# Router logits taken from the residual rows before their norm, with rows transposed one column half at a time

## What is computed

```
def rms_norm(x, gain):
    y = x32 * lax.rsqrt(jnp.mean(x32 * x32, axis=-1, keepdims=True) + EPS)
    return (y * gain.astype(jnp.float32)).astype(x.dtype)
...
        x = x + hybrid_mixer(h, ...)                 # ends with y @ w_out
        h = rms_norm(x, norm_ffn_gain[l])
        x = x + hierarchical_moe(h, w_router_group[l], b_router_group[l], w_router_expert[l], ...)
...
    group_p = jax.nn.softmax((t @ w_router_group) + b_router_group, axis=-1)
    exp_logits = ((t @ w_router_expert) + b_router_expert).reshape(n_tok, N_GROUPS, EXPERTS_PER_GROUP)
```

## Time and profile before

| | us |
|---|---|
| median of 3 runs (774.04, 775.37, 775.72) | 775.37 |
| the profiled execution, its own time | 773.31 |
| its span, first to last instruction | 771.6 |
| PE busy | 699.9 (91%) |
| VectorE busy | 334.7 (43%) |
| ScalarE busy | 288.7 (37%) |
| GpSimd busy | 199.5 (26%) |
| mean granted TensorE clock | 0.963 |

### The profile page before, as it was taken

One profiled execution on the slowest core, in us unless ns is written; L12 is line 12 of the kernel. 1 busy time (PEld: TensorE's weight loads), 2 busy tenths in 40 slices (PEclk: granted clock), 3 DMA queues, 4 the chain that ended last, 5 costly groups with the idle time before them and its releaser, 6 DMA issues.

```text
span 771.6 us, 10997 instructions
## 1 busy us (share of the span) xinstructions
PE 699.9 (91%) x4258; PEld 513.4 (67%) x4258; DVE 334.7 (43%) x612; ACT 288.7 (37%) x533; POOL 199.5 (26%) x171
## 2 busy tenths in 40 slices
PE   3999999998999999999999996699999999997830
PEld 3688888886878798888778886454455545454520
DVE  4349897979684423564478136500000000000008
ACT  6313655671444653565543131221222223131203
POOL 2045433431341231442552000212222121211110
PEclk9999999999999999999999996699999999999985
DMA  8913333030030020206741329889999999999726
GB/s 238 345 62 128 110 110 109 15 137 14 28 124 14 3 109 1 110 1 232 313 144 57 151 108 405 346 344 400 418 398 419 397 418 398 419 418 418 318 107 250
DMA packets 45122, 164.66 MB, mean 213 GB/s; under 512 B 9420, under 2 KB 13532, under 8 KB 32270
## 3 DMA queue, kind: packets, MB, share of 16 engines
q1 hardware_dynamic: 39758, 155.52, 52.1%
q0 software_dynamic: 5312, 8.42, 3.1%
HBM read 154.09 MB, written 19.53 MB: 225 GB/s over the span
## 4 chain that ended last, share of the span: by engine, by line
PE 82%; DVE 6%; ACT 4%; issue 3%; DMA 2%; POOL 2%; POOLq 0%; DVEq 0%; ACTq 0%
PE bank L961 14%; PE bank L467 13%; PE bank L469 12%; PE bank L468 12%; PE bank L995 7%; PE bank L958 5%; PE bank L940 3%; PE bank L989 2%; PE bank L595 2%; PE bank L972 2%; DVE arena L2364 1%; PE bank L858 1%; PE bank L626 1%; PE bank L616 1%; PE bank L798 1%
## 5 line engine op out<-in xcount | busy, mean ns | idle before, releaser
L1247 POOL TENSOR_TENSOR w_lo<-arena,w_hi 128x1024 fp32r<-128x1024 f32 x36 | 86.1, 2396 | 209.3 <-ACT w_hi L1410 209.3
L467 PE MATMUL bank<-h_hi,w_hi 128*128 128x512 f32 x320 | 128.3, 401 | 0.4 <-DVE arena L1953 0.4
L469 PE MATMUL bank<-h_hi,w_lo 128*128 128x512 f32 x320 | 125.0, 391 | 0.0
L468 PE MATMUL bank<-h_lo,w_hi 128*128 128x512 f32 x320 | 124.6, 389 | 0.0
L961 PE MATMUL bank<-arena 128*64 128x256 f32 x896 | 106.5, 392 | 8.4 <-issue 7.2
L961 PEld LDWEIGHTS bank<-arena 128*64 128x64 f32 x896 | 65.7, 140 | 39.0 <-issue 9.4
L2318 DVE TENSOR_TENSOR arena<-arena,bank 64x256 f32<-64x256 f32 x28 | 11.6, 412 | 180.8 <-ACT arena L1758 180.8
L1865 DVE SCALAR_TENSOR_TENSOR bank<-arena,bank 128x512 f32<-128x512 f32 x116 | 78.7, 749 | 0.1
L1371 POOL DMA_INDIRECT y_rows<-arena,row_half x28 | 28.0, 998 | 167.9 <-ACT arena L1779 167.9
L469 PEld LDWEIGHTS bank<-h_hi,w_lo 128*128 128x128 f32 x320 | 60.1, 188 | 13.1
L467 PEld LDWEIGHTS bank<-h_hi,w_hi 128*128 128x128 f32 x320 | 60.1, 188 | 12.9 <-DVE arena L1953 0.6
(11 more groups left out here) (355 smaller groups left out, 1131.7 us busy)
## 6 DMA issues: line engine op xcount, KB each, us to landing
arena<-in_w_expert_down_dram SPq DMA_DIRECT2D x33, 1024.0 KB, 20.7
arena<-in_w_expert_gate_dram SPq DMA_DIRECT2D x33, 1024.0 KB, 19.1
arena<-in_w_expert_up_dram SPq DMA_DIRECT2D x33, 1024.0 KB, 23.0
arena<-in_w_in_dram SPq DMA_DIRECT2D x8, 2048.0 KB, 8.1
arena<-in_x_dram SPq DMA_DIRECT2D x8, 512.0 KB, 7.3
arena<-in_w_in_dram SPq DMA_DIRECT2D x4, 1024.0 KB, 10.6
y_rows<-arena SPq DMA_DIRECT2D x8, 512.0 KB, 10.3
arena<-in_w_out_dram SPq DMA_DIRECT2D x2, 2048.0 KB, 10.2
```

The lines of the kernel that those rows point to most:

```text
L467: pe.matmul(o, wh, xh, start=first, stop=False)
L468: pe.matmul(o, wh, xl, start=False, stop=False)
L469: return pe.matmul(o, wl, xh, start=False, stop=last)
L1247: gp.tensor_tensor(as_raw(w_lo[pslot(s)], s), raw(s), as_raw(w_hi[pslot(s)], s).bitcast(F32), ALU.subtract)\
```

## The change

The logits are linear in the normed row, and the norm is one factor per token. So the changed kernel transposes the residual rows themselves, folds the gain into the router weights (one VectorE multiplication `wr * gcol`, with the gain loaded once more as a column per block of 128), and multiplies the finished logits by the reciprocal root, token by token (`logits_of`). Since a column half of a row is now enough for half of the transposes, PE transposes half tiles, `turn(c, half)`, behind the third product step (`m == 2`) of a later projection group in both passes, and multiplies whole tiles of logits behind the seventh (`m == 6`) in the second pass. ScalarE squares halves, and the sum of the first half enters the root as its bias. The normed rows `h2` are still made and stored, for the gather.

```diff
             def turn(c, half):
+                b = begin(("xT", c, half), copied(c, half))
+                wait(pe, "x1_ready", (1 - half) * NT + c + 1)
+                for k in range(KH):
+                    kk = half * KH + k
+                    ins = pe.transpose(b[:, k * P:(k + 1) * P], x1[:, c, kk * P:(kk + 1) * P], ident)
+                end(ins, ("xT", c, half), "route_mm")
+
+            def logits_half(c, half):
+                if half == 1:
+                    begin(("logits", c), ("x1_ready", NT + c + 2) if c < NT - 1 else ("routed", 1))
+                    held.append(jobs["logits", c][0])
+                    wait(pe, "wr_ready", 1)
...
+                for k in range(half * KH, half * KH + KH):
+                    ins = pe.matmul(b[:, 0:NL], h2T[:, k, c * P:(c + 1) * P], wr_wide[k],
+                                    start=(k == KH), stop=(k == KH - 1))
...
+                        if m == 2 and (p, c) != (0, 0):
+                            turn((c - 1) % NT, 1 if p == 0 or c == 0 else 0)
+                        if m == 6 and p == 1 and c > 0:
+                            logits_half(c - 1, 1)
+                            logits_half(c - 1, 0)
                     end(ins, ("wo", c, hf), "wo_mm")
-                    if p == 1 and c > 0:
-                        h2_tile(c - 1)
-                    if p == 1 and c > 1:
-                        logits_tile(c - 2)
-
-            logits_tile(NT - 2)
-            h2_tile(NT - 1)
-            logits_tile(NT - 1)
-            held.clear()
+            logits_half(NT - 1, 1)
+            turn(NT - 1, 0)
+            logits_half(NT - 1, 0)
...
-            sp.dma_start(wr[:, :, 0:NG], a["w_router_group"][0].rearrange("(p k) n -> p k n", k=KT)).then_inc(S["ld_part2"], 16)
-            sp.dma_start(wr[:, :, NG:NR], a["w_router_expert"][0].rearrange("(p k) n -> p k n", k=KT)).then_inc(S["ld_part2"], 16)
+            sp.dma_start(wr[:, :, 0:NG], a["w_router_group"][0].rearrange("(k p) n -> p k n", p=P)).then_inc(S["ld_part2"], 16)
+            sp.dma_start(wr[:, :, NG:NR], a["w_router_expert"][0].rearrange("(k p) n -> p k n", p=P)).then_inc(S["ld_part2"], 16)
+            sp.dma_start(gcol, a["norm_ffn_gain"][0].rearrange("(k p) -> p k", p=P), allow_slow_non_contiguous=True).then_inc(S["ld_part2"], 16)
...
-            v.wait_ge(S["ld_part2"], 48)
+            v.wait_ge(S["ld_part2"], 64)
+            TT(wr, wr, bc(gcol.unsqueeze(2), [P, KT, NR]), ALU.mult).then_inc(S["wr_ready"], 1)
             v.wait_ge(S["yc_mm"], KT)
...
+            def logits_of(c):
+                src = ready(v, ("logits", c))
+                return STT(out=lg[:, c, :], in0=src[:, 0:NR], scalar=sm["r2"][:, c:c + 1], in1=rbias,
+                           op0=ALU.mult, op1=ALU.add)
+
             for c in range(NT):
+                if c > 0:
+                    logits_of(c - 1)
                 add_half(c, 0)
...
-            tell(TT(lg, src[:, 0:NT * NL].rearrange("p (c n) -> p c n", c=NT)[:, :, 0:NR], bc(rbias.unsqueeze(1), [P, NT, NR]),
-                    ALU.add), "routed")
+            tell(logits_of(NT - 1), "routed")
```

More of the change, by code:

```diff
@@ L251, in hybrid_layer @@
         gain2 = at(R_S2, D)
+        gcol = g1
         gain3 = at(slot_at[HOME[3]], D)
@@ L827, in _ @@
                 end(ins, ("yd", m), "yd_mm")
-            def normed(c):
-                return "h2_ready", c + 1 + (c == NT - 1)
             def copied(c, half):
[L834 to L852, removed]
-                    wait(pe, "rconst", 1)
[L854 to L860, removed]
+                if half == 1:
+                    return "h2T_ready", c + 1
@@ new lines, in copied, with turn @@
+                return ("h2T_ready", NT + c + 1) if c < NT - 1 else ("h2_ready", NT)
+            def turn(c, half):
+                b = begin(("xT", c, half), copied(c, half))
[5 more added lines that the diff above has]
+            def logits_half(c, half):
+                if half == 1:
+                    begin(("logits", c), ("x1_ready", NT + c + 2) if c < NT - 1 else ("routed", 1))
+                    held.append(jobs["logits", c][0])
+                    wait(pe, "wr_ready", 1)
+                    wait(pe, "rconst", 1)
+                b = bank[jobs["logits", c][0]]
+                wait(pe, *copied(c, half))
+                for k in range(half * KH, half * KH + KH):
+                    ins = pe.matmul(b[:, 0:NL], h2T[:, k, c * P:(c + 1) * P], wr_wide[k],
+                                    start=(k == KH), stop=(k == KH - 1))
+                if half == 0:
+                    end(ins, ("logits", c), "route_mm")
+                    held.clear()
@@ L1164, in _ @@
             expert_dn(fixed[4], 4)
-            wait(sp, *jobs["logits"][1:])
+            wait(sp, *jobs["logits", NT - 1][1:])
             expert_dn(fixed[0], 0)
@@ L1714, in _, with xT_copy @@
             act.wait_ge(S["yc_ready"], 2 * KT)
[L1716 to L1732, removed]
+            def xT_copy(c, half):
+                tell(act.activation(h2T[:, KH * half:KH * half + KH, c * P:(c + 1) * P],
+                                    ready(act, ("xT", c, half)).rearrange("p (k n) -> p k n", k=KH), ACT.Copy),
+                     "h2T_ready")
+            for p, (hf, part) in enumerate(((1, "s1"), (0, "ss2"))):
+                for c in range(NT):
+                    act.wait_ge(S["x1_ready"], p * NT + c + 1)
+                    if p + c > 0:
+                        act.wait_ge(S["ss"], (p + 1) * NT + c)
+                    act.activation(junk[:, 0:HALF], x1[:, c, hf * HALF:(hf + 1) * HALF], ACT.Square,
+                                   accum_out=sm[part][:, c:c + 1]).then_inc(S["ss"], 1)
+                    if p == 1:
+                        act.wait_ge(S["ss"], 2 * NT + c + 1)
+                        if c == 0:
+                            act.wait_ge(S["x1_ready"], NT + 1)
+                            act.wait_ge(S["half_ss"], 1)
+                        act.activation(sm["ss2"][:, c:c + 1], sm["ss2"][:, c:c + 1], ACT.Sqrt, scale=1.0 / D,
+                                       bias=sm["s2"][:, c:c + 1]).then_inc(S["rms"], 1)
+                    if (p, c) != (1, NT - 1):
+                        xT_copy(c, hf)
             act.wait_ge(S["route_dif"], 1)
@@ L2350, in _ @@
             v.engine_nop().then_inc(S["ov_over"], 1)
-            v.wait_ge(S["ld_part2"], 64)
+            v.wait_ge(S["ld_part2"], 80)
             def final(c):
```

15 lines of the change are left out of this document (8 added, 7 removed).

## The result

The changed kernel takes 782.05 us (median of four runs, 781.43 to 782.59), the kernel before, on the same chip, 775.29 (774.04 to 775.72). The ratio is 1.0088 [1.0067, 1.0109]: **6.8 us slower**. The direction was forecast, the size was not: 2.7 us were predicted, and the range ended at 781.2.

A forecast was written before the change was run, and what follows sets the result against it. PE bounds the projection, expert-weight DMA the stretch from 510 to 711, with the routing deciding the end. Terms 5.3 + 1.4 - 4.0 = +2.7 us on the median 775.37 gave 778.1 us; range 774.8 to 781.2.

The forecast's parts named there:

- PE work in front of the last group, +5.3: Projection: more transposes and logits tiles on PE before its last group lengthen it by 5.3 us (4.8 to 5.8).
- the wait, +1.4: Projection's first pass: PE's first transposes wait for the first `add_half`, about 1.4 us (0.9 to 1.7).
- The rival that they would be hidden: Projection: moved PE work slips in cheaply between products; sum -2.6 to -1.0 us, 772.8 to 774.4 us; chance 0.15.
- The tail, -4.0: From the projection's last product to the selection: 4.1 us in place of 8.05, so -4.0 us (-3.4 to -4.4).
- The end of the run moves by what the selection's first instruction moves.: Routing to end: while the DMA queue still runs dry there, the run's end shifts as the selection does, +2.7 us.
- a rival with a chance of 0.10: First gather: sharing engines with more queued weights, it lands later, +3.0 us more, 781.1 us; chance 0.10.
- kept the queues full until the gather landed: Behind the projection: the nine weight loads filled the queues until the gather landed; they now wait 6.7 us longer.
- The +3.0 from the median of all gathers: First gather: if it took the median of all gathers, 8.9 us, in place of 5.92, +3.0 us more.
- The stream's floor, +1.8: Weight stream: loads 6.7 us later, 4.9 us of idle time absorbed; end at least 1.8 us later even without routing shift.
- the window 492 to 511: Around the first experts: sign to look for, DMA still runs dry once between 492 and 511 us.

The follow-up runs named there:

- no_stall: Changed kernel with the projection's first transposes behind the sixth product step instead of the third, where their sum is ready; 779.62 us, ratio 1.0056.
- before_hold2: Kernel before, with two weight loads (down of experts 0 and 4) issued behind the first gather's landing instead of in front of it; 775.73 us, ratio 0.9999.
- late_turns: Changed kernel with all transposes and logits behind the projection, except tile 0's transposes in its last group; copies on ScalarE; 772.87 us, ratio 0.9957.
- hold2: Changed kernel, with two weight loads (down of experts 0 and 4) issued behind the first gather's landing instead of in front of it; 777.06 us, ratio 1.0028.
- hold2_no_stall: Changed kernel with both edits: first transposes three product steps later, and two weight loads held behind the first gather; 777.40 us, ratio 1.0020.
- late_selection: Changed kernel with eight small VectorE additions, never read, in front of the selection; 781.19 us, ratio 1.0082.
- more_queued: Changed kernel with the three loads of expert 1 (3 MB) issued in front of the first gather instead of behind its landing; 779.89 us, ratio 1.0080.
- before_late_stream: Kernel before, with the nine weight loads after the projection issued behind the end of the logits instead of the last projection group; 778.89 us, ratio 1.0040.

## Why the prediction was right in direction and wrong in size

*PE work in front of the last group, +5.3, and the wait, +1.4.* Together 6.7; measured 6.55. The price of an insertion was right: of the 6.55, the wait took 1.37 to 1.58 (below), which leaves 5.0 to 5.2 for the moved work, and the chain has 0.44 for four transposes and 1.73 for a tile of logits. The rival that they would be hidden is refuted: its -1.0 at most against +2.31 at the selection. PE's last product before the first transposes, these, and VectorE's part of the wait:

```profile
422.81 0.39 PE L470 MATMUL bank<-wo_hi,ylo 128*128 128x512 f32 x1
...
424.56 0.63 PE L841 MATMUL bank<-arena 128*128 128x128 f32 x4 [1.37 <-DVE arena L2149]
```

```profile
418.81 4.63 DVE L2108 TENSOR_TENSOR wo_lo<-arena,wo_hi 128x1024 fp32r<-128x1024 f32 x4 [0.26 <-ACT wo_hi L1675]
...
423.37 0.45 DVE L2143 TENSOR_TENSOR arena<-arena 128x288 f32<-128x288 f32 x1
423.73 0.68 DVE L2149 TENSOR_TENSOR arena<-arena,bank 128x512 f32<-128x512 f32 x1
```

The idle time is 1.37 us, for 1.4 predicted; the new product `wr * gcol` took 0.45, for 0.4. In no_stall, without the wait, the last product came 1.58 earlier.

*The tail, -4.0.* From 469.53, where the chain leaves the projection (460.78 in the earlier trace rows), to the selection at 473.34 it is 3.81 us, for 4.1 predicted; the earlier trace rows show the same stretch of before.

```profile
469.56 0.69 DVE L2149 TENSOR_TENSOR arena<-arena,bank 128x512 f32<-128x512 f32 x1 [0.49 <-PE bank L470]
471.06 0.69 DVE L2170 COPY arena<-bank 128x512 f32<-128x512 f32 x1 [0.81 <-PE bank L841]
...
471.86 1.28 DVE L2175 SCALAR_TENSOR_TENSOR arena<-arena 128x1024 f32<-128x1024 f32 x1
473.06 0.25 DVE L2161 SCALAR_TENSOR_TENSOR arena<-bank,arena 128x36 f32<-128x36 f32 x1
473.34 0.17 DVE L2187 TENSOR_REDUCE arena<-arena 128x4 f32<-128x16 f32 x1
```

The normed row stands directly before the last logits, as foreseen. So the selection's shift, 6.55 - 4.24 = +2.31, was right within 0.4 us.

*"The end of the run moves by what the selection's first instruction moves."* **This step failed.** It held the gather's landing at 5.92 us, and priced the other case as a rival with a chance of 0.10. That rival was the truth: 9.45 us, +3.5. The argument against it was that "the slices around the first gather are full of weights before too, and it took 5.92 all the same". A slice of the page is 19 us long. Two-microsecond stretches would have shown that the share was falling to 0.74 as the gather landed. The sentence that the nine loads "kept the queues full until the gather landed" was wrong for the same reason: their queue was empty 2 us before. The prediction also had both numbers from which the collision follows, and did not set them against each other: the loads move 6.7 us and the gather 2.7, so 4.0 us of weights are added beside the gather. The +3.0 from the median of all gathers was the right size.

*The clock, which the sum did not have.* This is a second and smaller part. TensorE is granted half its clock (1.2 of 2.4 GHz) over the routing, and has it back some time after PE resumes. In the kernel before PE resumes at 489.68, and the clock rises at 496.7:

```profile
491.70:496.70 5.00, 3.90 (x20) 2.19 (x22) 2.59 (x14) 1.05 (x2) 0.93 (x1) 0.50 1.00 415
496.70:498.50 1.80, 1.80 (x17) 1.04 (x14) 0.00 (x0) 0.00 (x0) 0.00 (x0) 0.99 0.97 380
```

In the changed kernel it resumes at 497.71, and the clock rises at 506.6:

```profile
499.60:506.60 7.00, 5.83 (x29) 3.30 (x30) 0.00 (x0) 1.09 (x2) 0.93 (x1) 0.50 0.99 408
506.60:508.50 1.90, 1.82 (x16) 1.17 (x12) 0.00 (x0) 1.05 (x1) 0.00 (x0) 1.00 0.20 82
```

7.0 us there and 8.9 here; half of the difference, 0.91, shows in the chain as gate and up, 6.53 for 5.62. The prediction put this term at nothing without a word. Sum: 2.3 + 3.5 + 0.9 = 6.7, of the 6.8 measured. The first two terms are the change's. That the third is, isn't shown, and that the sum comes out so well is in part luck. The ten traces, in the order of the weights that moved beside the gather, show why:

| kernel | weights beside the first gather, MB | gather, us | from PE's resuming to the full clock, us | first gate and up, us |
|---|---|---|---|---|
| before_hold2 | 0 | 4.28 | 6.6 | 5.39 |
| late_turns | 0.55 | 4.31 | 7.5 | 5.83 |
| hold2 | 1.03 | 4.58 | 9.1 | 6.66 |
| hold2_no_stall | 1.07 | 4.85 | 8.6 | 6.40 |
| before | 1.34 | 5.92 | 7.0 | 5.62 |
| late_selection | 2.06 | 7.18 | 8.3 | 6.26 |
| more_queued | 3.07 | 8.53 | 6.1 | 5.17 |
| no_stall | 3.12 | 9.24 | 7.1 | 5.62 |
| changed | 3.15 | 9.45 | 8.9 | 6.53 |
| before_late_stream | 3.25 | 9.21 | 7.6 | 5.91 |

The gather's time follows the weights beside it. The first gate and up follows the clock, by half a microsecond for each one that it comes back later. The clock's return follows neither the gather nor the change: it takes 6.1 us in one kernel with the change and a long gather, and 9.1 in one with a short gather. There is one trace of each kernel, so how far it varies for one and the same kernel stays open.

*The stream's floor, +1.8.* It was not reached, so the weight stream itself did not set this kernel's end. DMA still runs dry once, as foreseen, in the stretch 514.20 to 516.60, which is 512.0 to 514.4 on the time axis of before's trace, outside the window 492 to 511 that I gave, since the experts came later:

```profile
514.20:516.60 2.40, 2.40 (x16) 1.02 (x14) 0.41 (x1) 0.77 (x2) 0.00 (x0) 1.00 0.00 0
```

before_hold2 shows that such a floor exists, there with two loads held back: the first expert came 1.7 us earlier, and the end did not move. How high it lies in the changed kernel, no run shows.

## What to carry to other kernels

When a change moves two releases by different amounts, write both shifts down and ask what now runs beside what: here the bulk loads moved by 6.6 us and the small gather that everybody waits for by 2.3, and the collision (3.5 us) cost more than the change's own sum (2.3). Read the queue's fill at the critical transfer in short stretches, not in the page's slices. Work inserted into a chain whose end releases bulk transfers can be paid twice, in the chain and in what the late transfers delay; put it behind that end, or hold back the loads that nobody needs yet until the critical transfer has landed.

## What the runs showed of the hardware that I had not expected

- The same gather takes 4.3 to 4.9 us where the weights end early and 8.5 to 9.5 where the engines stay full. Three megabytes more in the queue did not make it longer (8.53 for 9.45). Beside a full queue its first packet moves 4.3 to 4.4 us after its issue (in five traces), beside an empty one after 1.8.
- The granted clock returned 6.1 to 9.1 us after PE resumed, in ten traces, and the first gate and up took 5.17 to 6.66 us accordingly. A difference of 1.5 us between two single traces can come from that alone.
- The granted clock fell to 0.50 for a few us near 20 to 26 in eight of ten traces, and near 187 to 191 in three. It does not go with the change: before and more_queued had no such stretch, before_late_stream and the changed kernel had one. With a start that differs by 0.7 us, this makes the 3.3 us by which the projection's first product differs (413.35 to 416.61; 413.35 and 415.24 in two kernels that differ only behind it). Two traces are compared from a landmark behind such stretches.
